# A decoder step on one core: expert biases loaded when their home is free, the router in one block with the first slots ahead of the list, the second memory value product behind the second norm

## What is computed

```python
# memory attention of the prompt tokens
mk, mv = mem @ w_mk, mem @ w_mv                      # 256 x 512 each
q = rms_norm(h, norm_mem) @ w_mq
h = h + softmax(q mk^T / sqrt(128)) mv @ w_mo
# mixture of experts over all 264 tokens
tok = rms_norm(h, norm_ffn)
logits = tok @ router_w + router_b                   # 32 experts
vals, idx = top_k(logits, 4); gates = softmax(vals)  # combine: gate of each token and expert, else 0
for e in range(32):
    g, u = split(tok @ w_up[e] + b_up[e])
    act = min(g, 7) * sigmoid(1.702 * min(g, 7)) * (clip(u, -7, 7) + 1)
    acc += combine[:, e] * (act @ w_down[e] + b_down[e])
y = rms_norm(h + acc, norm_final)
```

## Time and profile before

| | |
|---|---|
| median of 3 runs | 1280.9 us (1277.92 to 1283.11) |
| the profiled execution | 1282.87 us, its span 1281.0 us |
| TensorE busy | 1185.7 us (93% of the span) |
| VectorE, ScalarE, GpSimd busy | 393.2, 226.8, 52.6 us |
| mean granted clock of TensorE | 0.967 of full speed |
| moved by transfers | 452.14 MB |

### The profile page before, as it was taken

How to read it: one execution, slowest core, us unless ns; L and a number is a source line. 1 busy time by engine, 2 the same in 40 slices (tenths; PEclk the granted TensorE clock), 3 DMA queues, 4 the chain that set the end, 5 groups by cost and what they waited for, 6 DMA issues and landing times.

```text
span 1281.0 us, 15525 instructions
## 1 busy us (share of the span) xinstructions
PE 1185.7 (93%) x6079; PEld 534.1 (42%) x6079; DVE 393.2 (31%) x933; ACT 226.8 (18%) x446; POOL 52.6 (4%) x67
## 2 busy tenths in 40 slices
PE   7997788898699999999899999999899999989997
PEld 5774555776333333333233333333333333333342
DVE  2376970343422222312122231322222231212222
ACT  1245541142201011110101111110101111110112
POOL 2127100000000000000000000000000000000000
PEclk9998699899699999999899999999999999999999
DMA  9234346407889999999999999999999999999993
GB/s 376 76 132 172 125 163 244 168 2 319 349 328 429 426 428 427 426 428 428 424 427 429 426 429 427 426 429 426 426 427 427 427 429 426 429 427 427 429 424 127
DMA packets 44220, 452.14 MB, mean 353 GB/s; under 512 B 5484, under 2 KB 6408, under 8 KB 18023
## 3 DMA queue, kind: packets, MB, share of 16 engines
q1 hardware_dynamic: 41711, 437.19, 81.6%
q0 software_dynamic: 2432, 13.89, 2.8%
HBM read 448.68 MB, written 2.61 MB: 352 GB/s over the span
## 4 chain that ended last, share of the span: by engine, by line
PE 69%; DVE 13%; DMA 13%; ACT 3%; issue 2%; POOL 0%; SPq 0%; DVEq 0%; ACTq 0%
PE psum L1196 26%; PE psum L1233 16%; DMA mem<-in_w_up_dram 10%; PE psum L1183 4%; PE psum L691 4%; DMA mem<-in_b_up_dram 3%; DVE mem L2089 2%; PE psum L1150 2%; PE psum L989 2%; PE psum L896 2%; DVE mem L2081 2%; DVE mem L2084 2%; PE psum L1174 1%; DVE mem L1879 1%; ACT mem L1614 1%
## 5 line engine op out<-in xcount | busy, mean ns | idle before, releaser
L1196 PE MATMUL psum<-mem 128*64 128x512 f32 x2048 | 460.3, 601 | 13.0 <-issue 6.3
L1196 PEld LDWEIGHTS psum<-mem 128*64 128x64 f32 x2048 | 144.6, 138 | 304.1 <-issue 291.2
L1233 PE MATMUL psum<-mem 128*64 128x512 f32 x1024 | 236.9, 600 | 0.0
L1233 PEld LDWEIGHTS psum<-mem 128*64 128x64 f32 x1024 | 66.6, 136 | 133.2 <-issue 112.6
L2081 DVE TENSOR_SCALAR mem<-psum 128x512 f32<-128x512 f32 x32 | 22.1, 691 | 271.2 <-PE psum L1196 271.2
L1614 ACT ACTIVATE mem<-mem 128x512 f32<-128x512 f32 x32 | 20.1, 629 | 471.1 <-DVE mem L2081 471.1
L1352 ACT ACTIVATE mem<-psum 128x512 f32<-128x512 f32 (+5 forms) x137 | 67.4, 546 | 149.3 <-PE psum L691 44.9
L2076 DVE TENSOR_TENSOR mem<-mem,psum 128x528 f32<-128x528 f32 x64 | 45.1, 704 | 145.9 <-PE psum L1183 145.9
L1183 PE MATMUL psum<-mem 128*128 128x264 f32 x256 | 65.5, 398 | 0.0
L2066 DVE TENSOR_SCALAR mem<-mem 128x64 f32<-128x64 f32 x102 | 25.6, 310 | 128.7 <-PE psum L1168 99.4
L1142 PE MATMUL psum<-mem 128*64 128x512 f32 x256 | 62.2, 607 | 2.4 <-DVE mem L2059 2.4
(11 more groups left out here) (313 smaller groups left out, 928.3 us busy)
## 6 DMA issues: line engine op xcount, KB each, us to landing
mem<-in_w_up_dram SPq DMA_DIRECT2D x128, 2048.0 KB, 29.4
mem<-in_w_down_dram SPq DMA_DIRECT2D x64, 2048.0 KB, 29.8
mem<-in_w_in_dram SPq DMA_DIRECT2D x8, 868.0 KB, 14.7
mem<-in_w_o_dram SPq DMA_DIRECT2D x1, 4096.0 KB, 14.2
mem<-in_cache_mem_k_dram SPq DMA_DIRECT2D x1, 4096.0 KB, 15.6
mem<-in_cache_mem_v_dram SPq DMA_DIRECT2D x1, 4096.0 KB, 14.9
mem<-in_w_mk_dram SPq DMA_DIRECT2D x1, 2048.0 KB, 8.6
mem<-in_w_mv_dram SPq DMA_DIRECT2D x1, 2048.0 KB, 13.6
```

What stands on the lines that cost most here:

```text
L1196: ins = pe.matmul(ps[64 * o:64 * o + 64, :], lhs, w[:, k % 2, g * 1024 + o * 512:g * 1024 + (o + 1) * 512], start=False, stop=(k == 7), sk ...
L1233: ins = pe.matmul(pso[64 * o:64 * o + 64, :], lhs, w[:, k % 4, o * 512:(o + 1) * 512], start=(k == 0), stop=(k == 7), skip_group_check=True)
```

## The change

It does four things.

1. mv 1 moves from ahead of the output projection to behind `ss 2` and the turns of the keys; its copy on ScalarE moves along, and with it the load of `w_mo` on SP and the stores of the values on POOL.
2. The two loads of `b_up` move in SP's queue from behind part 8 to behind `w_o`, after the pooling product (`pw 3`) is filled. `b_down` moves from SP's queue to POOL, behind the clear of its home.
3. The router handles its three blocks of rows in one instruction each where it can; the rows that a block of 8 leaves empty are cleared beforehand. The exponentials come after all six copies of `xr`. The positions are made first, then the slots of the first item (expert 0, base 0, which doesn't need the list), then gates and list. `gated` is cleared ahead of the router.
4. TensorE gathers the first item before the list is there; the products that spread the list and turn the gates stand behind the gather, in banks picked by hand, no longer as jobs. Before the loop TensorE now waits for the copy of the turned gates.

```diff
-    js += [("spv",), ("mv", 0), ("spo",), ("mv", 1)]
+    js += [("spv",), ("mv", 0), ("spo",)]
-    js += [("mkT", 0), ("mkT", 1), ("ss", 2)]
+    js += [("mkT", 0), ("mkT", 1), ("ss", 2), ("mv", 1)]
...
-    js += [("pos",), ("gT",), ("item",)]
+    js += [("pos",)]
     return js
...
             load(w_o_sb, w_o[0].rearrange("(k p) n -> p k n", p=P), "w_o_in")
+            wait_filled(sp, "pw", 3)
+            load(ybias[32:64, :], b_up[0, :, 0:D], "expert_bias_in")
+            load(ybias[64:96, :], b_up[0, :, D:2 * D], "expert_bias_in")
             wait_filled(sp, "mk", 1)
...
             load_part(8, 1)
-            load(ybias[32:64, :], b_up[0, :, 0:D], "expert_bias_in")
-            load(ybias[64:96, :], b_up[0, :, D:2 * D], "expert_bias_in")
-            sp.wait_ge(S("rows_zero"), 1)
-            load(outb[0:NE, :], b_down[0], "down_bias_in")
             for r in range(3):
...
             pool.memset(outb, 0.0).then_inc(S("rows_zero"), 1)
+            pool.wait_ge(S("rows_zero"), 1)
+            pool.dma_start(outb[0:NE, :], b_down[0]).then_inc(S("down_bias_in"), 16)
             pool.wait_ge(S("stored_small"), 16 * 11)
...
             done(ins, "spo")
-            memory_product("mv", 1, w_mv_sb)
...
             sum_squares(2)
+            memory_product("mv", 1, w_mv_sb)
             pe.wait_ge(S("w_mq_in"), 16)
...
             b = take(pe, "pos")
-            pe.wait_ge(S("masks_ready"), 3)
+            pe.wait_ge(S("masks_ready"), 1)
             for r in range(3):
...
             done(ins, "pos")
-            b = take(pe, "gT")
-            pe.wait_ge(S("gates_ready"), 3)
-            for r in range(3):
-                ins = pe.transpose(b[0:NE, r * P:r * P + ROWS[r]], meta[0:ROWS[r], r, 1, :], ident[0:ROWS[r], 0:ROWS[r]])
-            done(ins, "gT")
-            b = take(pe, "item")
-            pe.wait_ge(S("items_found"), 2)
-            pe.matmul(b[:, 0:LIST], ones, diag_e, start=True, stop=True)
-            done(pe.matmul(b[:, 128:128 + LIST], ones, diag[:, 0:LIST], start=True, stop=True), "item")
-
             psx, psx_t, psa_t, psh0, psh1, pso, psy0, psy1 = banks
+            held = number[("pos",)] % 8
+            assert held in (5, 6, 7)
+            gate_bank, item_bank = [banks[n] for n in (2, 5, 6, 7) if n != held][:2]
             for n in range(8):
-                last = max(v for v in number.values() if v % 8 == n)
-                pe.wait_ge(S(f"drained{n}"), last // 8 + 1)
+                if n != held:
+                    last = max(v for v in number.values() if v % 8 == n)
+                    pe.wait_ge(S(f"drained{n}"), last // 8 + 1)
-            for r in range(3):
-                for g in range(2):
-                    wait_drained(pe, "xr", r, g)
             gather_prompts(1)
             gather_samples_and_bias()
+            pe.wait_ge(S("items_found"), 2)
+            pe.matmul(item_bank[:, 0:LIST], ones, diag_e, start=True, stop=True)
+            pe.matmul(item_bank[:, 128:128 + LIST], ones, diag[:, 0:LIST], start=True, stop=True
+                      ).then_inc(S("items_spread"), 1)
+            turn_tokens(1)
+            pe.wait_ge(S("gates_ready"), 1)
+            for r in range(3):
+                ins = pe.transpose(gate_bank[0:NE, r * P:r * P + ROWS[r]], meta[0:ROWS[r], r, 1, :],
+                                   ident[0:ROWS[r], 0:ROWS[r]])
+            ins.then_inc(S("gates_turned"), 1)
             pe.wait_ge(S("down_bias_in"), 16)
-            turn_tokens(1)
+            wait_drained(pe, "pos")
+            pe.wait_ge(S("st_copied"), 1)
             pe.wait_ge(S("list_ready"), 3)
...
-            for t in range(2):
-                b = result(act, "mv", t)
-                copy(mv[:, t, :], b[:, :], "mv", t)
+            b = result(act, "mv", 0)
+            copy(mv[:, 0, :], b[:, :], "mv", 0)
             squares(2, "wo")
...
+            b = result(act, "mv", 1)
+            copy(mv[:, 1, :], b[:, :], "mv", 1)
...
-                act.wait_ge(S("top_ready"), r + 1)
-                act.activation(expr[0:w, r, :], lgr[0:w, r, :], ACT.Exp, bias=small[0:w, 8 + r:9 + r]
-                               ).then_inc(S("exp_r"), 1)
...
-            b = result(act, "gT")
-            act.wait_ge(S("st_zero"), 1)
-            act.activation(ST[0:NE, :], b[0:NE, 0:NT], ACT.Copy).then_inc(drained("gT"), 1)
-            wait_drained(act, "gT")
-            act.sem_inc(S("st_copied"), 1)
+            act.wait_ge(S("top_ready"), 1)
+            for r in range(3):
+                w = ROWS[r]
+                act.activation(expr[0:w, r, :], lgr[0:w, r, :], ACT.Exp, bias=stat[0:w, r:r + 1]).then_inc(S("exp_r"), 1)
             copy_tokens(1)
             copy_turned(1)
+            act.wait_ge(S("gates_turned"), 1)
+            act.wait_ge(S("st_zero"), 1)
+            gate_bank = [banks[n] for n in (2, 5, 6, 7) if n != number[("pos",)] % 8][0]
+            act.activation(ST[0:NE, :], gate_bank[0:NE, 0:NT], ACT.Copy).then_inc(S("st_copied"), 1)
             act.wait_ge(S("list_ready"), 3)
             dve.tensor_scalar(smp, smp, stat[:, 33:34], None, ALU.mult).then_inc(S("smp_ready"), 1)
+            dve.memset(at(temp_off + NT * 0, 480), 0.0).then_inc(S("dve_step"), step())
             b = result(dve, "smT")
...
+            three = at(small_off + 8, 3, 8)
+            negmax, cnt3, need3 = stat[:, 0:3], stat[:, 4:7], stat[:, 8:11]
+            flat = "p r e -> p (r e)"
+            dve.wait_ge(S("stored_small"), 16 * 11)
+            dve.wait_ge(S("stored_un"), 32)
+            dve.memset(gated, 0.0).then_inc(S("dve_step"), step())
+            dve.wait_ge(S("dve_step"), steps[0])
             b = result(dve, "rl")
-            for r in range(3):
-                w = ROWS[r]
-                ins = dve.tensor_tensor(lgr[0:w, r, :], b[0:w, r * NE:(r + 1) * NE], rb_sb[0:w, :], ALU.add)
-            ins.then_inc(drained("rl"), 1)
+            dve.tensor_tensor(lgr[0:TS, 2, :], b[0:TS, 2 * NE:3 * NE], rb_sb[0:TS, :], ALU.add).then_inc(S("dve_step"), step())
+            dve.tensor_tensor(lgr[:, 0:2, :], b[:, 0:2 * NE].rearrange("p (r e) -> p r e", r=2),
+                              rb_sb.unsqueeze(1).to_broadcast([P, 2, NE]), ALU.add).then_inc(drained("rl"), 1)
+            dve.wait_ge(S("dve_step"), steps[0])
             wait_drained(dve, "rl")
             for r in range(3):
-                w = ROWS[r]
-                link(dve.max(top8[0:w, :], lgr[0:w, r, :]))
-                dve.tensor_scalar(small[0:w, 8 + r:9 + r], top8[0:w, 0:1], -1.0, None, ALU.mult).then_inc(S("top_ready"), 1)
-                ties(lgr[0:w, r, :], top8[0:w, 3:4], TOPE, maskr[0:w, r, :], seler[0:w, r, :], cumr[0:w, r, :],
-                     small[0:w, 0:1], small[0:w, 1:2])
-                dve.tensor_tensor(maskr[0:w, r, :], maskr[0:w, r, :], cumr[0:w, r, :], ALU.add
-                                  ).then_inc(S("masks_ready"), 1)
-            dve.wait_ge(S("masks_ready"), 3)
+                dve.max(three[:, r, :], lgr[:, r, :]).then_inc(S("dve_step"), step())
+            dve.wait_ge(S("dve_step"), steps[0])
+            dve.tensor_scalar(negmax, three[:, :, 0], -1.0, None, ALU.mult).then_inc(S("top_ready"), 1)
+            fourth = three[:, :, 3:4].to_broadcast([P, 3, NE])
+            dve.tensor_tensor(seler, lgr, fourth, ALU.is_equal).then_inc(S("dve_step"), step())
+            link(dve.tensor_tensor(maskr, lgr, fourth, ALU.is_gt))
+            dve.tensor_reduce(cnt3, maskr, AX.X, ALU.add).then_inc(S("dve_step"), step())
+            dve.wait_ge(S("dve_step"), steps[0])
+            v = seler.rearrange(flat)
+            link(dve.tensor_tensor_scan(cumr.rearrange(flat), v, v, 0.0, ALU.add, ALU.max))
+            dve.wait_ge(S("dve_step"), steps[0])
+            link(dve.tensor_scalar(need3, cnt3, -1.0, float(TOPE), ALU.mult, ALU.add))
+            link(dve.tensor_tensor(need3[:, 1:3], need3[:, 1:3], cumr[:, 0:2, NE - 1], ALU.add))
+            link(dve.tensor_tensor(cumr, cumr, need3.unsqueeze(2).to_broadcast([P, 3, NE]), ALU.is_le))
+            link(dve.tensor_tensor(cumr, cumr, seler, ALU.mult))
+            dve.tensor_tensor(maskr, maskr, cumr, ALU.add).then_inc(S("masks_ready"), 1)
+            dve.wait_ge(S("masks_ready"), 1)
             dve.wait_ge(S("late_tables_in"), 16)
-            link(dve.memset(meta, -1.0))
+            dve.tensor_scalar(esel, const("part32", SLOTS), 0.0, None, ALU.is_equal)
+            link(dve.memset(meta, 0.0))
+            b = result(dve, "pos")
+            dve.scalar_tensor_tensor(out=meta[:, 0:2, 0, :], in0=b[:, 0:2 * NE].rearrange("p (r e) -> p r e", r=2),
+                                     scalar=1.0, in1=maskr[:, 0:2, :], op0=ALU.add, op1=ALU.mult).then_inc(S("dve_step"), step())
+            dve.scalar_tensor_tensor(out=meta[0:TS, 2, 0, :], in0=b[0:TS, 2 * NE:3 * NE], scalar=1.0,
+                                     in1=maskr[0:TS, 2, :], op0=ALU.add, op1=ALU.mult).then_inc(S("dve_step"), step())
```

(49 more changed lines are left out.)

4 lines of the change are left out of this document (added).

## The result

The changed kernel takes 1267.9 us (median of 5 runs, 1265.22 to 1271.75) against 1280.9 (5 runs, 1277.92 to 1283.11): ratio 0.99, interval 0.9875 to 0.9925, so 13.0 us less. The forecast was 1264.0 (range 1259 to 1273) from a sum of 16.9 us. The profiled execution took 1265.22 us, span 1263.2, with a mean granted clock of 0.973 (before 0.967); it is 17.8 us of span shorter, but it was the quickest of its five runs.

What follows compares the result with a forecast made beforehand. The prediction took the stream of expert weights, with its late start and 13.2 us empty, to bound the kernel. Gains of 5.2 + 10.9 + 0.8 = 16.9 us off the median 1280.9 gave 1264.0 us, range 1259 to 1273.

Steps and rivals of the forecast that it cites:

- the hole ahead of 356 us: Expert stream, 348 to 356 us: next to nothing moves, 7.9 us lost; 13.2 us empty in all, recoverable at the end.
- Part 1: mv 1 behind the second norm fills TensorE's idle time, keeps the clock high; expert stream starts 5.2 us earlier.
- first release: First expert part given back sooner after the first expert product starts: another 0 to 1.6 us, taken as 0.8.
- Part 2: Router: positions product 1.25 us earlier, right behind the tokens' turns; slots made first, so the gather starts 9.7 us earlier.
- Part 3: From gather to first expert product, with biases already there: first product 10.9 us earlier, bounds 9.2 and 11.8.
- Part 4: Down bias on POOL's own queue: goes out at about 325.1, lands at 332 to 334, free.
- rival (a): Down bias lands late, at 346.1, first expert product 3.1 us earlier only: gain 8.3, 1272.6 us; chance 0.13.
- Rival (b): Stream's hole isn't worth anything, only its earlier start counts: 1275.7 us; chance 0.09 together with (c).
- (c): Change does not do what it says, neither part moves the stream: 1280.9 us; chance 0.09 together with Rival (b).
- (d): Expert stream's rate falls below 419 GB/s from 427, making the kernel slower, 1288 us or so; chance 0.04.

Runs made afterwards that it cites:

- changed kernel again: The changed kernel, unedited, run again for a second profile and more times: 1268.24 us, ratio 0.989 against the kernel before.
- the biases alone: Kernel before with only b_up loaded behind w_o and b_down loaded on POOL: 1278.88 us, ratio 0.9973.
- the rest alone: Changed kernel with mv 1 back at its old place ahead of the output projection: 1270.28 us, ratio 0.9899 against the kernel before.
- Part 1 alone: Kernel before with only mv 1, its job and its copy moved behind the second norm: 1275.13 us, ratio 0.9936.
- filler: Kernel before plus an unread product of 8 instructions between ss 2 and the query product: 1281.58 us, ratio 0.9998.
- the run without the wait: Changed kernel without TensorE's wait for the copy of the turned gates ahead of the loop: 1264.68 us, ratio 0.987 against the kernel before.
- the early parts: Changed kernel with expert parts 0 to 3 issued as soon as their homes are free: 1265.6 us, ratio 0.9867 against the kernel before.
- The late start: Changed kernel plus six products on TensorE ahead of the expert loop, their result overwritten: 1269.42 us, ratio 0.9915 against the kernel before.
- the two without the wait: Changed kernel without the turned-gates wait ahead of the loop, 1264.68 us, and the same with parts 0 to 3 issued early, 1265.94 us.
- more work: Changed kernel plus one overwritten product per pair of experts on TensorE in the loop: 1272.62 us, ratio 0.9909 against the kernel before.

## Why the prediction was right, and where its sum was off

The step that mattered held: the end hangs on the stream, and the hole ahead of 356 us is worth its length. The gain comes out through the marks of the trace; the median has 13.0 of the 16.9 us, within the range.

| term | predicted | marks, after | changed kernel again |
|---|---|---|---|
| Part 1, stream starts earlier (S - M) | 5.2 | 4.3 | 5.5 |
| the same from E (S - E) | 5.2 | 5.5 | 5.5 |
| Parts 2, 3 and first release (F - S) | 11.7 | 11.8 | 11.9 |
| sum, from M | 16.9 | 16.05 | 17.3 |
| sum, from E | 16.9 | 17.3 | 17.35 |
| median | 16.9 | 13.0 | 14.1 |

**Part 1.** The product took the idle stretch, the clock stayed at 2.4 GHz, and the query product is 14.40 us. Predicted 14.3. From E it is worth 5.5 us at S in both traces; the 4.3 from M comes from the slower mv 0 of one of them. The base is a single trace, though: laid against the trace of the biases alone (S - E 86.80) it is 4.4, against that of the rest alone (87.73) 5.35. What was not foreseen is that the clock further on changes too. These are windows of the third norm, the router product and the turns `xr`, laid to the same work in both traces, in the columns of the earlier trace rows. Before:

```profile
309.00:315.17 6.17, 2.02 (x9) 1.12 (x8) 3.21 (x5) 1.01 (x3) 0.00 (x0) 1.00 1.00 430
315.17:323.02 7.85, 7.85 (x49) 7.68 (x49) 2.69 (x7) 0.00 (x0) 0.00 (x0) 0.50 1.01 432
323.02:327.03 4.01, 4.01 (x26) 3.56 (x24) 3.55 (x24) 2.57 (x4) 0.96 (x1) 0.70 1.04 437
```

After:

```profile
303.15:309.32 6.17, 2.02 (x9) 1.11 (x8) 3.21 (x5) 1.01 (x3) 0.00 (x0) 0.89 1.01 433
309.32:317.21 7.89, 7.88 (x48) 7.72 (x48) 3.06 (x8) 0.00 (x0) 0.00 (x0) 0.50 1.01 432
317.21:322.15 4.94, 4.94 (x29) 4.46 (x27) 3.33 (x17) 2.78 (x5) 1.48 (x2) 0.56 1.00 421
```

The clock falls at this norm in both, where TensorE idles for 4 us of 6.2. But after the change it falls sooner (0.89 against 1.00 in the norm), is lower in the turns (0.56 against 0.70), and the turns take 0.9 us more. In all the kernels with mv 1 moved or the stretch filled they take 4.8 to 5.2 us, in the three others 3.8 to 4.0. Why the fall comes at another moment, no run settles. What it costs depends on what stands behind. With the old router (Part 1 alone, filler) the turns are hidden behind the masks, and the first expert product pays 0.8 to 1.0 us. With the new router the turns are what is waited for; yet with mv 1 at its old place, where the turns and the gather are quick (3.92 and 1.94 us), the first expert product takes 5.35 us in place of 3.65, and F - S is 48.22 against 48.14 and 48.05. So in the changed kernel all 5.4 us of Part 1 reach F, and alone it is 4.5. That these clock terms cancel was not foreseen, and is luck.

**Part 2.** The masks are ready at 320.81, behind S by 31.5 us (predicted 31.0), and the positions follow the turns at once, as said. The gather comes 3.46 us after them (predicted 3.5), at 325.45 (predicted 325.4): 9.0 of the 9.7 us; the longer turns took the rest.

**Part 3.** From the gather to the first product 8.12 us, predicted 8.2; the first product starts at 333.57, predicted 333.6. The size is right by errors that cancel. The gather took 3.38 at the lower clock, near the upper bound (3.7), and the way into the loop 1.41 us, where I took 0.6, called it the reading of the count and gave it bounds of 0 to 1.2 that no row showed; the run without the wait shows that 1.3 of the 1.99 idle us belong to the added wait. Against that, the products and copies between them were quicker than taken. Counted from S, the first product comes 10.3 us earlier than before, not 10.9. The first 16 instructions then take 3.65 us, at full rate, and the first release comes 3.84 us after the first product (before 5.33): 1.5 gained, 0.8 taken. So 10.3 + 1.5 stands where 10.9 + 0.8 was forecast, and that the sum fits to 0.1 us is luck.

**Part 4 and rival (a).** 7.4 us to landing, within the 8 predicted. The 21.0 us of the same bytes were a matter of the queue: in SP's queue they took 19.6 us again, on POOL's 7.4. POOL cleared the rows in 0.96 us and issued in 0.52 while VectorE was at the router, and between issue and landing no instruction of VectorE lasted over 0.36 us. The Trainium skill's rule on the port that GpSimd and VectorE share ("SBUF — State Buffer", section "SBUF: two separate sides") has the port taken for one whole instruction at a time, and by some instructions only. To make it the whole of rival (a) was to read too much into it; whether it cost a part of the 7.4 us, no run here shows. The prediction also misread its rows on one point: the first two stores of POOL (186.94) did not go out beside an idle VectorE, but beside four of its copies from PSUM (186.65 to 189.96). Rival (a)'s price was 8.6 us; in the run it was 8.9 from S to F and 5 to 6 by the ratios.

**Rival (b)**, only the stream's start counts, is refuted: the rest alone gains 13.0 us with the stream's start where it was, and the early parts move the start and gain nothing from M or E to F. The late start says the same, but in its trace alone. **(c)** and **(d)** fell with the result: 427 GB/s throughout. In one point the prediction's wording was off. It said "whatever starts the stream earlier or fills its hole comes out at the end". An earlier start alone doesn't: what comes out is F, as long as the ring is full before it. In eleven of fourteen traces span - F lies between 925.6 and 926.1 us, with F - S from 48.1 to 64.2 (and with parts 0 to 3 issued early); the other three are the two without the wait and the one with more work. Part 1 is worth what it is because everything behind it, F too, moves along.

**The median** is 3 to 4 us short of the sum. Part of it is the choice of trace: the profiled execution of before lay 0.7 us from the median of its runs in the later jobs (51 runs, 1276.35 to 1287.20, median 1282.18), those of after 2.7 and 3.3 below theirs. So the 17.8 us between two profiled executions is not what the medians differ by. What is different inside the slower executions of the changed kernel, no trace shows, since each was taken from the quickest run of its group; their lower mean clock (0.969) is all that is known. The nearest hint is in two other kernels that were traced in slower executions, the rest alone (1273.72, the slowest of its four) and more work (1272.61): they reach E at 209.97 and 208.61, 1.7 to 3.2 us later than the changed kernel's two traces, and from E to F run as the others do (F - E 135.95 and 130.62). So a good part of the scatter may stand ahead of all that was changed; for the changed kernel itself that is not shown.

## What to carry to other kernels

In a stream through a ring of buffers, look up the moment at which the first buffer is given back, and count from there to the end: if that stretch is constant, only what moves that moment counts, and loads issued earlier don't. Two waits that end together (a late load and a late router) are worth little one by one; price them together, and move a small load out of the queue in which the big ones stand. When the hole is closed, little is left there: in single traces the next microsecond needed two edits. And put the mark from which traces are compared right ahead of the changed code: 29 us of untouched work between them hid 1.2 us of the gain here.

## What the runs showed of the hardware that was not expected

- The same 128 KB landed in 7.4 us from POOL's queue and in 19.6 to 22.0 from SP's, with the transfer engines as full (share 1.02 and 392 GB/s in the changed kernel from 319.0 to 326.4, 1.00 and 411 GB/s with the bias back on SP from 319.0 to 338.6); the two loads of 128 KB of `b_up` behind nine parts took 34 to 36 us.
- Keeping the clock at 2.4 GHz in one stage (250 us) gave 2.8 us there and moved the moment of the next fall, some 55 us later, by a little: 24 turns that neither edit had touched took 4.8 to 5.2 us in place of 3.8 to 4.0. With filler alone, 1.5 of the 2.8 us were gone by F.
- A wait of 7.9 us ahead of a product of 16 instructions went with a granted clock of 0.54 in that product, which took 6.58 us against 3.65 at 1.00.
- A wait for a copy of 0.37 us, placed ahead of a read of the loop count, cost 1.3 us of idle time there, although the loop waits for the same copy again further on.
